# A MoE decoder step: half of each expert's down weights land in a staging area, and the gated sum is formed ahead of the last round

## What is computed

```
v = h * (1 + scale2) + shift2
f = moe_ffn(v)                     # top 4 of 32 experts, softmax gates
y = layer_norm(DEEPNORM_ALPHA * h + gate2 * f, ln2_g, ln2_b)

def expert_block(xb, e):
    hh  = xb @ w_up[e] + b_up[e]           # 1024 -> 2048
    act = glu * sigmoid(1.702 * glu) * (lin + 1)
    return act @ w_down[e] + b_down[e]     # 1024 -> 1024
```

## Time and profile before

| what | value |
|---|---|
| median of 3 runs | 1293.86 us |
| the profiled execution's own time | 1293.17 us |
| its span, first to last instruction | 1291.3 us |
| PE busy | 1202.0 us (93%) |
| DVE, ACT, POOL busy | 564.5, 255.9, 161.3 us |
| bytes moved by DMA | 466.33 MB |
| mean granted TensorE clock | 0.974 |

### The profile page before, as it was taken

How to read it: one execution, slowest core, us unless ns; L and a number is a source line. 1 busy time by engine, 2 the same in 40 slices (tenths; PEclk the granted TensorE clock), 3 DMA queues, 4 the chain that set the end, 5 groups by cost and what they waited for, 6 DMA issues and landing times.

```text
span 1291.3 us, 17054 instructions
## 1 busy us (share of the span) xinstructions
PE 1202.0 (93%) x5960; PEld 520.4 (40%) x5961; DVE 564.5 (44%) x1059; ACT 255.9 (20%) x404; POOL 161.3 (12%) x96
## 2 busy tenths in 40 slices
PE   5999999979899999989999999999999999999991
PEld 2588886523333333333333333333333333333330
DVE  0407906764443443334443443433444434434457
ACT  1523210242121211111111211211211212111121
POOL 0456452044200000000000000000000000000024
PEclk9899999879899999999999999999999999999995
DMA  9866696459999999999996999997899999699961
GB/s 350 312 248 264 247 304 236 141 222 420 400 425 427 425 427 425 426 425 426 426 411 270 427 426 426 428 426 325 356 428 427 426 427 427 265 423 427 425 257 41
DMA packets 54732, 466.33 MB, mean 361 GB/s; under 512 B 5463, under 2 KB 5623, under 8 KB 18585
## 3 DMA queue, kind: packets, MB, share of 16 engines
q1 hardware_dynamic: 52761, 460.11, 86.7%
q0 software_dynamic: 1952, 5.97, 1.4%
HBM read 464.29 MB, written 1.77 MB: 361 GB/s over the span
## 4 chain that ended last, share of the span: by engine, by line
PE 63%; DMA 26%; DVE 7%; ACT 1%; POOL 1%; issue 1%; SPq 1%; DVEq 0%; ACTq 0%; POOLq 0%
PE bank L899 26%; DMA ring<-in_w_up 24%; PE bank L933 12%; PE bank L685 8%; PE bank L875 3%; PE bank L736 3%; DMA ring<-in_w_in 2%; PE bank L753 2%; PE bank L800 2%; PE bank L671 2%; PE bank L924 1%; DVE front L1397 1%; PE bank L629 1%; ACT front L1090 1%; POOL front L539 1%
## 5 line engine op out<-in xcount | busy, mean ns | idle before, releaser
L899 PE MATMUL bank<-ring,front 128*64 128x512 f32 x2240 | 505.9, 597 | 22.1 <-DMA ring<-in_w_up 22.1
L899 PEld LDWEIGHTS bank<-ring,front 128*64 128x64 f32 x2240 | 153.0, 137 | 317.2 <-issue 269.5
L933 PE MATMUL bank<-ring,front 128*64 128x512 f32 x1120 | 250.0, 599 | 7.0 <-ACT front L1090 7.0
L1370 DVE TENSOR_TENSOR front<-front,bank 128x512 f32<-128x512 f32 (+1 forms) x210 | 143.9, 685 | 57.4 <-PE bank L875 35.7
L1356 DVE TENSOR_TENSOR O_parts<-bank,O_parts 64x512 fp32r<-64x512 f32 x70 | 48.2, 689 | 239.1 <-ACT O_parts L1056 234.6
L933 PEld LDWEIGHTS bank<-ring,front 128*64 128x64 f32 x1120 | 77.8, 138 | 155.3 <-issue 141.5
L1087 ACT ACTIVATE front<-front 128x256 f32<-128x256 f32 x70 | 29.2, 417 | 505.1 <-DVE front L1388 505.1
L571 POOL TENSOR_TENSOR parts_home<-front 128x1024 f32<-128x1024 f32 (+1 forms) x2 | 5.2, 2577 | 918.1 <-DVE onehot_T L1411 918.1
L1388 DVE TENSOR_SCALAR front<-bank 128x256 f32<-128x256 f32 x70 | 29.7, 424 | 165.2 <-PE bank L899 163.9
L875 PE MATMUL bank<-O_parts,onehot_T 128*128 128x512 f32 x216 | 81.1, 454 | 10.5 <-DVE front L1436 6.3
L1056 ACT ACTIVATE O_parts<-bank 64x512 fp32r<-64x512 f32 x70 | 41.4, 592 | 237.0 <-PE bank L933 236.2
(11 more groups left out here) (217 smaller groups left out, 875.9 us busy)
## 6 DMA issues: line engine op xcount, KB each, us to landing
ring<-in_w_up SPq DMA_DIRECT2D x128, 2048.0 KB, 18.7
ring<-in_w_down SPq DMA_DIRECT2D x128, 1024.0 KB, 17.8
ring<-in_w_ada SPq DMA_DIRECT2D x12, 2048.0 KB, 11.9
ring<-in_w_in SPq DMA_DIRECT2D x8, 2048.0 KB, 8.3
ring<-in_w_o SPq DMA_DIRECT2D x2, 2048.0 KB, 21.4
hx<-in_x_prompt SPq DMA_DIRECT2D x2, 1024.0 KB, 7.9
ring<-in_w_out_a SPq DMA_DIRECT2D x1, 2048.0 KB, 7.7
ring<-in_w_out_b SPq DMA_DIRECT2D x1, 2048.0 KB, 7.4
```

The lines of the kernel that those rows point to most:

```text
L899: last = mm(bank[B_UP[j]][64 * h:64 * h + 64, :], x_T[:, (c % 2) * 2 + b, 64 * (c // 2):64 * (c // 2) + 64], w[:, :, at:at + 256], start=F ...
L933: last = mm(bank[B_DOWN][64 * h:64 * h + 64, :], act_T[:, 2 * j + b, 64 * hh:64 * hh + 64], expert_chunk_at(UP_CHUNKS + m)[:, b * 1024 + h ...
L1370: signal(TT(Y[0:r, 2 * t + h, :], Y[0:r, 2 * t + h, :], bank[b][0:r, :], ALU.add), bank_free[b], value)
```

## The change

It does four things. (1) Chunks 6 and 7 of every expert but the first no longer land in the ring but in `stage`, a separate 2 MiB region, whose old contents (the rows of `v` and what followed them) are dead by then. POOL copies `stage` into the ring slot once the expert before has used that slot (`move_staged`), and signals `staged_ready`; PE waits for that signal ahead of chunk 6, and SP waits for it before it loads `stage` again. (2) POOL's work on `h` is interleaved with the first three copies, and each tile now waits for the end of a round's DVE work; the gain and offset of the second norm are loaded at the end of the kernel and not at its start. (3) `Y = gate2 * Y + h` is formed on DVE for all three tiles ahead of the last round. (4) The last round is written out once more on DVE, with the share multiplied by `gate2` into a buffer `share` and then added to `Y`; the tail's code reads `Y` and `share`.

```diff
+STAGED = UP_CHUNKS + 2
...
+        stage = region(front, 0, CH)
+        norm1_gain, norm1_offset = region(front, 4096, D), region(front, 12392, D)
+        gate2_rows = (norm1_gain, norm1_offset)
+        share = region(front, 8292, 2, 512)
...
-            with sp.Fori(1, E) as e:
-                rounds_done = sp.value_load(table[0:1, bass.ds(e + 127, 1)], min_val=1, max_val=52)
-                for c in range(EXPERT_CHUNKS):
+            def stage_chunks(e):
+                for c in range(STAGED, EXPERT_CHUNKS):
+                    src = a["w_down"][0].rearrange("e (m p b) n -> p e m (b n)", m=DOWN_CHUNKS, p=P)[:, e, c - UP_CHUNKS]
+                    sp.dma_start(stage[:, (c - STAGED) * 2048:(c - STAGED + 1) * 2048], src).then_inc(staged_landed, 16)
+            def next_expert(e, rounds_done):
+                for c in range(STAGED):
...
                     expert_chunk(c, e)
+                    if c == UP_CHUNKS - 1 and isinstance(e, int) and e == 1:
+                        sp.wait_ge(v_part_ready, len(PARTS))
+                        sp.wait_ge(b_up_ready, 1)
+                        stage_chunks(1)
+            next_expert(1, sp.value_load(table[0:1, 128:129], min_val=1, max_val=52))
+            sp.wait_ge(staged_ready, 2)
+            stage_chunks(2)
+            with sp.Fori(2, E - 1) as e:
+                next_expert(e, sp.value_load(table[0:1, bass.ds(e + 127, 1)], min_val=1, max_val=52))
+                sp.wait_ge(staged_ready, e + 1)
+                stage_chunks(e + 1)
+            next_expert(E - 1, sp.value_load(table[0:1, E + 126:E + 127], min_val=1, max_val=52))
...
+            def move_staged(e):
+                rounds_done = pool.value_load(table[0:1, bass.ds(e + 127, 1)], min_val=1, max_val=52)
+                pool.wait_ge(staged_landed, 32 * e)
+                pool.wait_ge(bank_full[B_DOWN], rounds_done + front_uses(B_DOWN))
+                pool.tensor_tensor(mark[0:1, 1:2], mark[0:1, 0:1], mark[0:1, 0:1], ALU.add)
+                pool.tensor_copy(ring[:, EXPERT_SLOT[UP_CHUNKS + 1], :], stage).then_inc(staged_ready, 1)
...
             for i, t in enumerate(TILE_ORDER):
+                move_staged(i + 1)
                 pool.wait_ge(row_normed, i + 1)
+                pool.wait_ge(onehot_ready, i + 3)
...
-            pool.dma_start(tail_rows[:, 2 * D:3 * D], a["ln2_g"][0].partition_broadcast(P)).then_inc(tail_landed, 16)
-            pool.dma_start(tail_rows[:, 3 * D:], a["ln2_b"][0].partition_broadcast(P)).then_inc(tail_landed, 16)
...
+            with pool.Fori(4, E) as e:
+                move_staged(e)
+            pool.wait_ge(staged_ready, E)
+            pool.wait_ge(expert_landed[UP_CHUNKS - 1], 16 * E)
+            pool.dma_start(tail_rows[:, 2 * D:3 * D], a["ln2_g"][0].partition_broadcast(P)).then_inc(norm2_landed, 16)
+            pool.dma_start(tail_rows[:, 3 * D:], a["ln2_b"][0].partition_broadcast(P)).then_inc(norm2_landed, 16)
...
-                    pe.wait_ge(expert_landed[UP_CHUNKS + m], e * 16 + 16)
+                    if UP_CHUNKS + m < STAGED:
+                        pe.wait_ge(expert_landed[UP_CHUNKS + m], e * 16 + 16)
+                    else:
+                        pe.wait_ge(staged_ready, e + 1)
...
+            def share_of(n, t, h):
+                b = B_C[h]
+                value = n * PER_ROUND[b] + (front_uses(b) + t + 1)
+                dve.wait_ge(bank_full[b], value)
+                signal(TT(share[0:ROWS[t], h, :], bank[b][0:ROWS[t], :], gate2(t, h), ALU.mult), bank_free[b], value)
+            def add_share(n, t):
+                for h in range(2):
+                    share_of(n, t, h)
+                    row = Y[0:ROWS[t], 2 * t + h, :]
+                    step(TT(row, row, share[0:ROWS[t], h, :], ALU.add))
...
-            with dve.Fori(1, G) as g:
+            with dve.Fori(1, final) as g:
                 low_of_result(g, bank[B_DOWN])
                 round_work(g)
...
+            dve.wait_ge(tail_landed, 16 * (1 + NSEQ))
             dve.wait_ge(h_ready, 3)
+            for t in range(3):
+                r = ROWS[t]
+                rows = Y[0:r, 2 * t:2 * t + 2, :].rearrange("p h d -> p (h d)")
+                step(TT(rows, rows, (gate2_rows[t // 2])[0:r, :], ALU.mult))
+                step(TT(rows, rows, hx[0:r, t, :], ALU.add))
...
+            low_of_result(final, bank[B_DOWN])
+            round_work(final, add=add_share)
...
-                step(TT(out_rows[:, 0, h * 512:(h + 1) * 512], Y[:, h, :], gate2(0, h), ALU.mult))
-            step(TT(out_rows[:, 0, :], out_rows[:, 0, :], hx[:, 0, :], ALU.add))
...
                 if t < 2:
-                    normalise(r)
+                    normalise(r, meanwhile=lambda: share_of(G, t + 1, 0))
```

More of the change, by code:

```diff
@@ L214, in program @@
         O_parts = nc.alloc_sbuf_tensor_at("O_parts", [P, 2, 512], F32R, offset=start + 4 * (RING * CH + 11368))
+        mark = region(small, 672, 4)
         w_pool = region(small, 160, 4, P)
@@ L247, in program @@
         expert_used = [sem(f"expert_used{c}") for c in range(EXPERT_CHUNKS)]
+        staged_landed = sem("staged_landed")
+        staged_ready = sem("staged_ready")
         const_landed = sem("const_landed")
@@ L531, in _ @@
             pool.memset(Y, 0.0).then_inc(cleared, 1)
+            pool.wait_ge(expert_landed[STAGED], 16)
+            pool.wait_ge(expert_landed[STAGED + 1], 16)
+            pool.memset(mark[0:1, 0:1], 0.0).then_inc(staged_ready, 1)
             pool.wait_ge(bank_full[B_X], front_uses(B_X) + 1)
@@ L1429, in _ @@
                 r = ROWS[t]
-                if t:
-                    dve.wait_ge(sum_ready, t)
                 for h in range(2):
-                    i, b = 2 * t + h, B_C[h]
-                    value = G * PER_ROUND[b] + (front_uses(b) + t + 1)
-                    dve.wait_ge(bank_full[b], value)
-                    signal(TT(Y[0:r, i, :], bank[b][0:r, :], gate2(t, h), ALU.mult), bank_free[b], value)
-                    share = Y[0:r, i, :]
+                    if h or not t:
+                        share_of(G, t, h)
                     half = out_rows[0:r, t, h * 512:(h + 1) * 512]
-                    step(TT(half, half, share, ALU.add))
+                    step(TT(half, Y[0:r, 2 * t + h, :], share[0:r, h, :], ALU.add))
                     step(v.bn_stats(stats[0:r, 6 * h:6 * h + 6], half))
                 if t < 2:
-                    normalise(r)
+                    normalise(r, meanwhile=lambda: share_of(G, t + 1, 0))
+            dve.wait_ge(norm2_landed, 32)
             r, row = ROWS[2], out_rows[0:ROWS[2], 2, :]
```

54 lines of the change are left out of this document (22 added, 32 removed).

## The result

The changed kernel takes **1306.35 us** (median of 4 runs, 1303.04 to 1307.73), the kernel before 1293.84 us beside it (4 runs, 1291.06 to 1295.07). The ratio is 1.0094, with a 95% interval of 1.0081 to 1.0106: slower by 12.5 us, and outside the predicted range of 1288 to 1302. The profiled execution is the fastest of the four: 1303.04 us, span 1300.9 us, against 1293.17 us and 1291.3 us before, so the trace has 9.6 us to explain and the medians somewhat more.

What follows compares the result with a forecast made beforehand. The prediction took the weight stream as the bound with one round per expert, PE in the double rounds. Terms 4.92 - 3.5 + 1.4 + 2.0 + 0.4 - 2.45 - 0.8 gave +2.0 on 1293.17: 1295.1 us, range 1288 to 1302.

Steps and rivals of the forecast that it cites:

- Order of the stream: SP's weight stream: chunks 6 and 7 go ahead of the next expert's up chunks, delaying these by 2 MiB; +4.92 us, once.
- Gap at the start: First staged pairs: SP's queue runs dry while expert 2's pair waits for handover, copy and lag; +1.4 us (0 to 3).
- Second norm's loads: Gain and offset loads leave the stretch around 340 us for a time when DMA is free; -3.5 us (-2.5 to -4.3).
- Gaps after the doubles: After the second rounds of experts 13 and 20 the queue runs dry waiting for the copy; +1.0 us each, +2.0.
- POOL's work on `h`: Early rounds: the work moves into the down matmuls and its delay goes, but PE then waits for the stream; 0.
- The empty window in the doubles: Second round of expert 13: the DMA window of some 13 us stays as empty as before, 11.7 us idle.
- It just fits: Ahead of the last round: six DVE operations on Y finish in time, and the last copy waits for the sixth; +0.4 us.
- rival C: Ahead of the last round: POOL's copy takes the ports before the sixth operation on Y, PE loses 2.8 us; 1297.5 us; chance 0.14.
- Rival B: POOL's copy is slow, deciding from about 4.6 us a copy: 1300.5 us at 6 us each, 1311.6 at 9.7; chance 0.12.
- Tail: After the last down matmuls: the split no longer waits for DVE, -2.45 us, and next tiles' first shares fill square-root waits, -0.8.

Runs made afterwards that it cites:

- with the port freed: The changed kernel with POOL's last copy (expert 31) held until DVE's six operations on Y are done; 1298.38 us, and 1300.0 us when run again.
- the second one: The changed kernel itself, unaltered, run again on one chip beside other kernels; 1305.42 us, ratio 1.0101 to the kernel before.
- the control: The changed kernel with only SP's loop over experts written out 31 times; 1306.01 us.
- slow-copy: The changed kernel with each POOL copy made as a two-input operation, times a column of ones; 1320.19 us, ratio 1.0231 to the kernel before.

## Why the prediction was wrong, step by step

The sum named the right places, and missed the median by 11.3 us and the profiled execution by 7.9. One term, +0.4 for the six operations on Y, took the wrong one of two outcomes; four others were off in size by 1 to 2 us each, and all to the same side. By terms:

- **Order of the stream, +4.92: right as far as can be told** (4.75 are left when the dry queue is taken off), as was the reason that it is paid once. With the gap at the start, the first stage grows by 7.1 us against the kernel without staging (7.4 with the port freed).
- **Gap at the start, +1.4: 2.65 us.** The copy is 3.59 us where I took 4.2; the Trainium skill (GPSIMD Engine Reference, section 3.1), with an estimate of 3.5, was nearer. The error is in "only 4, 5 are left in the queue (4.92 us)". POOL, released by the landing, starts at 312.68, and bytes flow again 1.8 us after SP's issue at 316.43. So with 2.65 us of dry queue they had run out at about 318.2 - 2.65 = 315.6: only 2.9 us of transfers were left. The windows of 1 us agree: after 312.68 only 1.2 MB more flow before the queue is dry, and chunks 4 and 5 are 2.1 MB. So they had moved in part before the pair was complete.
- **Second norm's loads, -3.5: -1.8 to -2.6.** I took the middle of two bounds, where the bytes (2.5) were the better end. The slower stream at 340 us, my reason for more than the bytes, belongs in the main to the loads of `gate2`, which stayed.
- **Gaps after the doubles, +1.0 each, +2.0: too small.** The windows behind the first double show 2.1 us of dry queue. By stages it is +0.82 and +2.49 in the profiled execution, +2.34 and +1.24 in the second one, +1.65 and +3.97 in the control, +0.26 and +1.30 with the port freed and +0.54 and +1.40 there again: sums of 1.6 to 5.6 us, with a spread that no run here explains.
- **POOL's work on `h`, 0: right.** By the starts of the down matmuls the second and the third round now each come 27.05 us after the one before, where it was 31.2 and 29.1, and the first stage is the same with and without it. The empty window in the doubles was right too.
- **The failed step: "It just fits", +0.4.** I had the copy due 0.2 us ahead of the sixth operation and took the case in which it waits for that one. POOL won, in each of the four traces of this kernel or its unrolled and slow-copy twins, by 0.03 or 0.04 us, and in each the copy begins within 0.01 us of the end of the fifth operation. By my own times POOL was due while the fifth ran, and what counted was that it already waited when the fifth ended. The fourth stage grew by 3.39 us in the profiled execution and by 5.66 in the second. The place and mechanism are rival C's, and its price of 2.8 us is near the 3.39 of the trace. What it left out is the clock: in the second execution, in the control and with the slow copy it fell behind this wait. The rule of the Trainium skill (SBUF — State Buffer, section "SBUF: two separate sides") that whoever starts first holds the pair agrees: the operation ends at 1243.38, after the copy's end at 1242.30. By it, who starts first should have been the question, and my own numbers spoke for POOL; a chance of 0.14 was too low. C's price alone would still have given 1297.5: the measured 1306.35 lies outside the range because the other terms were short as well.
- **Rival B is out**: at 3.59 us the copy is below the 4.6 from which it decides.
- **Tail, -3.25: -1.87.** The split starts 0.66 us after the down matmuls (1269.38) where before it was 3.12: the -2.45 is right. But the second add of the next tiles now falls beside POOL's norm. DVE's timeline has, and before the change had,

```profile
1280.02 1.95 DVE L1493 TENSOR_TENSOR parts_home<-front 128x512 f32<-128x512 f32 x1
...
1287.24 1.97 DVE L1493 TENSOR_TENSOR parts_home<-front 64x512 f32<-64x512 f32 x1
```

```profile
1271.39 1.18 DVE L1439 TENSOR_TENSOR parts_home<-parts_home,front 128x512 f32<-128x512 f32 x1
```

  So they take 1.95 and 1.97 us where before the same adds (L1439) took 1.18 each; these 1.6 us eat the -0.8 and more.

The sum with what was measured, in the profiled execution: +5.28 + 0.82 + 2.49 + 3.39 - 1.87 = +10.1, less 0.5 for the earlier start. In the second one, where the clock fell: +4.83 + 2.34 + 1.24 + 5.66 - 1.87 = +12.2, less 0.8, nearer to the 12.5 us of the medians.

## What to carry to other kernels

A prefetch through a staging buffer helped here only in a window in which the queue is idle; elsewhere, put ahead of what the engine waits for next, it was a delay, and 2 MiB of it is 4.92 us. Before pricing such an idle window, work out the next bound: here PE left 2 to 3 us of 4.9. A copy on POOL cost not its length but what it met: with 31 copies each time and the port freed, the three places of the pair in the stream, and so of the copy among DVE's operations with two SBUF operands, gave 1298, 1313 and 1329 us. And where two engines are due within some tenths of a microsecond, ask which of them already waits when the operation ahead ends, and put both outcomes in the forecast with their full price.

## What was not expected of the hardware

- A wait of PE for DVE of 2.13 us was followed by the lower clock (0.50, 16 matmuls in 5.94 us) in one execution and by full clock (3.65 us) in another of the same program, on another chip. The same delay of DVE cost 3.2 us with the clock up and 5.4 with it down.
- A POOL operation of 128 x 4096 with a constant column as second input took 7.00 us, 1.71 ns an element, against 2426 ns for 1024 elements, 2.37 ns each, with two full inputs.
- A copy on POOL that was released while a DVE operation with two SBUF operands ran began at that operation's end, ahead of the next one of DVE, in four of four traces (1238.71 against 1238.72 us in the first).
- The start of the stream moves by 6.5 us between executions (276.0 to 282.5 us). The first stage of the changed kernel agrees within 0.5 us in three executions, the next two only within 1.5 and 2.7, so a difference of 1 or 2 us there says little.
